# A gated DeltaNet stage: decay sums computed a tile ahead, modulation blocks in four places, inverse blocks moved over two queues

## The chip, the cores and the metric

The kernel runs on one core of a Trainium2 chip. The metric is the device time of one execution in microseconds; before the change the median of three runs is 2671.44 us (2667.06 to 2678.87). Engines: PE or TensorE (matmul), DVE or VectorE, ACT or ScalarE, POOL or GpSimd, SP or SyncE (which issues most DMAs).

## The reference, cut to what matters

One inference step of a two-layer model on 128 context and 512 latent tokens, D_MODEL 1024, float32. Layer 0 mixes by a bidirectional gated DeltaNet (4 heads of 128) beside differential attention, then a dense SwiGLU; layer 1 by latent attention, then experts. Every sub-layer is modulated by vectors `silu(c) @ mod_w + mod_b`. The change touches the DeltaNet and the products with `mod_w`:

```python
g = jnp.cumsum(g, axis=-1)
gdiff = g[..., :, None] - g[..., None, :]
decay = jnp.where(incl, jnp.exp(jnp.where(incl, gdiff, 0.0)), 0.0)
m = jnp.where(strict, jnp.einsum('bhncd,bhnsd->bhncs', kb, k) * decay, 0.0)
a = m + jnp.eye(CHUNK)
sol = lax.linalg.triangular_solve(a, rhs, lower=True, unit_diagonal=True)   # -> u, w
def step(s, inp):                       # over chunks, once forward, once backward
    v_new = u_i - w_i @ s
    o = (q_i * jnp.exp(g_i)) @ s + a_i @ v_new
    s = s * jnp.exp(g_last) + k_dec.T @ v_new
m_s = jnp.split(jax.nn.silu(c) @ mod_w[layer] + mod_b[layer], 6)
```

## The kernel before, in words

The 640 tokens are five tiles of 128 (`NT`), and each tile is one chunk. The inverse of the triangular matrix of each of 2 directions x 5 tiles x 4 heads is made in four steps.

1. *Tile loop* (`pe_delta`, `dve_delta`, `act_delta`, `pool_delta`). GpSimd copies the log decays of a tile over 128 columns (`rows_of`, L1004, one buffer `gb`); TensorE sums them by a product with a triangle ("grow", L1066), transposes keys and values ("tok", L1070 and L1072) and makes both grams ("gram"). VectorE makes the exponents (`exponents`, L1195: L1198, L1203), ScalarE takes exp (L1156), GpSimd multiplies by beta (L1019), and VectorE multiplies into the grams (L1215, L1219); with L1219 the gram's PSUM slot is free. GpSimd also adds up a mask `diag` from ten pieces (L1011, L1012).
2. *Substitution* (`substitute`, L1039). The 32x32 diagonal blocks (4 per matrix, 160 in all) go through DRAM (`z_dram`, L457, then L463) so that each of 80 partitions holds one; VectorE inverts those of direction 0 and GpSimd those of direction 1, in 31 steps of two products (L1046, L1048).
3. *Way back.* The inverses go to `x_dram` (L466, L1024) and come back by `bring_back` (L469, issue at L474), in 20 DMAs of 16 KB for each direction, SyncE's and GpSimd's. VectorE widens them by `diag` (`widen`, L1259), TensorE transposes (`pe_turn`, L1122), and two levels of products (5 and 6) complete the inverse of each tile.
4. *Scan* (`pe_scan`, `dve_scan`), five steps, and the output norm (`pe_onorm` and its partners), then the out projection "eo" with weights `w_eo`.

The order is written out by hand in lists: `TRI` for steps 1 to 3, `STEP` for a scan step. Every entry is one use of a ring of four PSUM slots, in list order; `take` makes TensorE wait until the entry four back was freed, `full` and `done` wait for an entry to be written or freed. An engine runs its own instructions in program order only.

Between them stand the *modulation blocks*: 40 blocks (0 to 39) of 1 MB of `mod_w`. Block b is an entry ("mA", b), eight narrow products of which ScalarE copies the result (L1138), and an entry ("mB", b), a fold and its bias (L1143). Before, blocks 0 to 4 lie in the tile loop, one to a tile, blocks 5 to 29 behind it (`MOD_SCAN` 30), two in each scan step (30 to 39). Their weights come through a ring of five SBUF slots (`WS`), loaded by SyncE in order (L436), each as soon as the block five back was consumed. SyncE's other work hangs on these loads (`carry`, L446): behind load 4 it sends 12 MB of zeros to `rows_dram` (L450), behind loads 4 to 8 a tile's diagonal blocks (L457, eight DMAs), behind load 8 it reads them back (L463), and behind load 22 (`X_BACK`) it waits for the inverse of direction 0, sends it and brings it back. Loads 23 and later wait in program order behind that.

## Time and profile before

| | |
|---|---|
| profiled execution | 2674.86 us (span 2672.9 us) |
| median of three runs | 2671.44 us |
| TensorE busy, whole span | 2367.9 us, 89% |
| VectorE, ScalarE, GpSimd busy | 38%, 32%, 17% |
| DMA | 353.62 MB, mean 132 GB/s |
| tile loop | about 449 to 521 us |
| substitution | 529 to 571 us |
| inverse back, until TensorE's first turn | 571 to 609.5 us |
| levels 5 and 6, and the scan | 609.5 to 749 us |
| output norm, out projection starts | 749 to 763 us |

The profile gives, for one execution, each engine's instructions with start and length, what ended the wait before them, and the DMA issues with their time to landing. Busy time over a whole span says little about a stage in which engines hand work to each other: there one reads who was waited for last. "PEclk" is the granted TensorE clock as a share of the full 2.4 GHz. The ends of matmuls are modelled.

### The profile page before, as it was taken

To read this page: it belongs to the slowest core of one execution; us is meant where nothing else is said; L and a number is where in the kernel's file an instruction comes from. 1 tells how busy PE (TensorE), PEld (TensorE's weight loads), DVE (VectorE), ACT (ScalarE), POOL (GpSimd) and SP (SyncE) were. 2 spreads that over 40 slices of the span, in tenths; PEclk is the share of its full clock that TensorE was granted. 3 is DMA by queue.
4 is the path that set the end of the run, shared out by engine and by line. 5 is a ranking of instruction groups with operands and counts; after the bars stand their busy time and mean duration, and the time that the engine had idled before them with its cause. 6 is when DMAs were issued, how large, how long until landed. Compare 5 with 4: busy or idle time off the path is not lost.

```text
span 2672.9 us, 34343 instructions
## 1 busy us (share of the span) xinstructions
PE 2367.9 (89%) x13870; PEld 1987.9 (74%) x13871; DVE 1005.9 (38%) x1457; ACT 868.2 (32%) x1237; POOL 450.2 (17%) x249
## 2 busy tenths in 40 slices
PE   6999986578888999989989999969898888898994
PEld 3777665447767999989966566769797777797883
DVE  2211264354742222131112333133345766634544
ACT  2211234222104211131122232134335666644544
POOL 0000001273002000020000000024224444433311
PEclk7998988758999999999999999969999999999997
DMA  6111102672310222111211000016448778866755
GB/s 284 49 63 48 40 32 101 212 297 101 134 62 34 81 78 79 65 44 66 107 43 50 17 1 1 0 68 260 165 155 291 292 290 302 321 237 212 264 176 173
DMA packets 72890, 353.62 MB, mean 132 GB/s; under 512 B 15056, under 2 KB 20752, under 8 KB 40112
## 3 DMA queue, kind: packets, MB, share of 16 engines
q1 hardware_dynamic: 68368, 337.94, 34.5%
q0 software_dynamic: 4384, 13.60, 1.4%
q8 instruction: 116, 1.90, 0.3%
q14 instruction: 22, 0.18, 0.0%
HBM read 318.06 MB, written 33.46 MB: 132 GB/s over the span
## 4 chain that ended last, share of the span: by engine, by line
PE 63%; issue 15%; DVE 9%; POOL 7%; ACT 4%; DMA 2%; SPq 1%; POOLq 0%; DVEq 0%; ACTq 0%
PE ps L543 59%; POOL wring_x L1801 5%; PE ps L680 1%; PE ps L898 1%; DVE tmp L1048 1%; ACT arena L950 1%; DVE tmp L1046 1%; DMA xT<-in_x 1%; POOL arena_x L1512 1%; DVE att L920 1%; DVE tmp L1319 1%; DVE tmp L1259 0%; POOL rows L1984 0%; ACT hT L671 0%; DMA wring<-in_w_mod 0%
## 5 line engine op out<-in xcount | busy, mean ns | idle before, releaser
L543 PE MATMUL ps<-hT,wring 128*128 128x320 f32 x1472 | 406.5, 439 | 12.6 <-ACT hT L671 10.6
L543 PEld LDWEIGHTS ps<-hT,wring 128*128 128x128 f32 x1472 | 284.4, 194 | 134.6 <-issue 20.6
L1801 POOL TENSOR_TENSOR wring_x<-wring,arena_x 128x2048 fp32r<-128x2048 f32 (+1 forms) x60 | 276.7, 4619 | 495.6 <-ACT arena_x L1795 495.5
L543 PE MATMUL ps<-arena_x,hT_x 128*128 128x256 f32 x2464 | 330.3, 292 | 21.1 <-issue 21.1
L543 PEld LDWEIGHTS ps<-arena_x,hT_x 128*128 128x128 f32 x2464 | 312.5, 197 | 24.5 <-issue 22.6
L1795 ACT ACTIVATE arena_x<-wring 128x2048 fp32r<-128x2048 f32 x153 | 283.4, 1855 | 90.6 <-DMA wring<-in_w_mgu 89.8
L543 PE MATMUL ps<-arena_x 128*128 128x512 f32 (+2 forms) x1144 | 252.3, 374 | 29.5 <-DVE arena_x L1970 13.3
L1801 DVE TENSOR_TENSOR wring_x<-wring,arena_x 128x2048 fp32r<-128x2048 f32 (+1 forms) x90 | 222.1, 2467 | 73.1 <-ACT arena_x L1795 73.0
L543 PEld LDWEIGHTS ps<-arena_x 128*128 128x128 f32 x1144 | 203.0, 201 | 59.9 <-issue 25.5
L543 PE MATMUL ps<-arena 128*128 128x128 f32 (+3 forms) x680 | 184.3, 434 | 7.0 <-ACT arena L950 4.8
L543 PE MATMUL ps<-wring_x,hT_x 128*128 128x256 f32 x1120 | 151.9, 285 | 5.0 <-POOL wring_x L1801 4.9
L543 PEld LDWEIGHTS ps<-arena 128*128 128x128 f32 (+1 forms) x680 | 107.8, 224 | 62.7 <-issue 48.4
L543 PEld LDWEIGHTS ps<-wring_x,hT_x 128*128 128x128 f32 x1120 | 142.4, 193 | 6.0 <-POOL wring_x L1801 5.7
L543 PE MATMUL ps<-tmp_x,arena_x 128*128 128x320 f32 x832 | 135.3, 315 | 6.0 <-ACT hT L671 6.0
L543 PE MATMUL ps<-hT_x,arena_x 128*128 128x320 f32 x832 | 132.4, 310 | 0.7 <-POOL hT_x L1553 0.7
L543 PEld LDWEIGHTS ps<-tmp_x,arena_x 128*128 128x128 f32 x832 | 127.8, 192 | 6.5 <-issue 6.5
L543 PE MATMUL ps<-tmp_x,wring_x 128*128 128x320 f32 x832 | 131.2, 310 | 0.0
L543 PEld LDWEIGHTS ps<-hT_x,arena_x 128*128 128x128 f32 x832 | 124.9, 188 | 1.0 <-POOL hT_x L1553 1.0
L543 PEld LDWEIGHTS ps<-tmp_x,wring_x 128*128 128x128 f32 x832 | 124.3, 188 | 0.1
L1934 ACT ACTIVATE expf<-ps 128x256 f32<-128x256 f32 x110 | 42.1, 383 | 232.8 <-PE ps L543 232.6
L1406 DVE SCALAR_TENSOR_TENSOR xT<-ps,modcol,xT 128x128 f32<-128x128 f32 (+2 forms) x72 | 27.2, 434 | 226.1 <-PE ps L543 226.1
L2024 DVE TENSOR_TENSOR expf<-expf,ps 128x256 f32<-128x256 f32 x110 | 45.7, 416 | 149.1 <-ACT expf L1934 149.1
(288 smaller groups left out, 2890.9 us busy)
## 6 DMA issues: line engine op xcount, KB each, us to landing
wring<-in_w_mgu SPq DMA_DIRECT2D x105, 1024.0 KB, 6.0
wring<-in_w_mod SPq DMA_DIRECT2D x48, 1024.0 KB, 9.9
wring<-in_w_mdn SPq DMA_DIRECT2D x30, 1024.0 KB, 5.0
wring<-in_w_gu SPq DMA_DIRECT2D x22, 1024.0 KB, 4.8
wring<-in_w_mdn SPq DMA_DIRECT2D x20, 768.0 KB, 4.3
wring<-in_w_ev SPq DMA_DIRECT2D x14, 1024.0 KB, 5.3
rows<-hT SPq DMA_DIRECT2D x1, 12288.0 KB, 33.5
wring<-in_w_dn SPq DMA_DIRECT2D x16, 704.0 KB, 4.2
```

The source lines that it names most:

```text
L543: return nc.tensor.matmul(out, lhsT, rhs, start=first, stop=last)
L680: last = nc.tensor.matmul(pair(s)[:, half, :], ones, tc[:, k, half * HT:(half + 1) * HT], start=(k == 0), stop=(k == KD - 1))
L898: last = nc.tensor.transpose(ps[:, s, n * P:(n + 1) * P], probs(i, 0)[:, n * P:(n + 1) * P], ident)
L920: nc.vector.tensor_reduce(cells(i)[:, st_:st_ + 1], src, AX.X if t == 0 else AX.XY, ALU.max, negate=True).then_inc(mx_ready, 1)
L950: nc.scalar.activation(dst, src, ACT.Exp, bias=cells(i)[:, st_:st_ + 1], accum_out=cells(i)[:, 2 + st_:3 + st_]).then_inc(ps_free[s], 1)
L1046: st.then(eng.tensor_tensor(part, L[:, k + 1:B32, k:k + 1].broadcast_to([NB, rest, n]), X[:, k:k + 1, 0:n].broadcast_to([NB, rest, n]), AL ...
L1048: last = eng.tensor_tensor(X[:, k + 1:B32, 0:n], X[:, k + 1:B32, 0:n], part, ALU.subtract)
L1406: last = nc.vector.scalar_tensor_tensor(xs, ps[:, s, at:at + b - a], modcol[:, bass.ds(c * 2 + (gate * 16 + grp), 1)], xs, ALU.mult, ALU.add)
L1795: nc.scalar.activation(whi[b % 6][:, 0:wsize(b)], wslot[s][:, 0:wsize(b)], ACT.Copy).then_inc(whi_ready, 1)
L1801: eng.tensor_tensor(wslot_x[s][:, 0:size], wslot[s][:, 0:size], whi[b % 6][:, 0:size].bitcast(F32), ALU.subtract).then_inc(ready, 1)
L1934: nc.scalar.activation(sgE[:, j % 2, :, :], pair(s, P), ACT.Silu).then_inc(silu_ready, 1)
L2024: nc.vector.tensor_tensor(actf[:, j % 2, :, :], sgE[:, j % 2, :, :], ps[:, s, :].rearrange("p (m n) -> p m n", m=2)[:, :, P:2 * P], ALU.mu ...
```

## The change

- *Decay sums a tile ahead.* ("grow", t+1) now comes between ("tok", t) and ("gram", t) on TensorE; ScalarE's exp of tile t+1 follows the token copy of tile t; GpSimd copies the rows of tile 1 before it adds up `diag`, and those of tile t+2 behind its beta products of tile t.
- *Modulation blocks over four places.* Two blocks to each tile of the loop (0 to 9), 10 to 24 behind it, 25 to 34 in the scan, and 35 to 39 in a new stage "omod" between the scan and the output norm. VectorE's three `modA` products move behind the norm's own.
- *Transfers.* Of each tile's diagonal blocks SyncE sends direction 0 (behind loads 4, 6, 8, 10, 12) and GpSimd direction 1, four DMAs each; each reads its own direction back, on a semaphore of its own (SyncE behind load 14). The way back has eight DMAs for each direction: for each row group g one of tiles 0 to 3 (64 KB) and one of tile 4 (16 KB), with `compact` laid out to match. `X_BACK` is 27.

```diff
-MOD_SCAN = 30
+MOD_TRI, MOD_SCAN, MOD_END = 10, 25, 35
-X_BACK = 22
+X_BACK = 27
-        TRI = [x for t in range(NT) for x in (("grow", t), ("tok", t), ("gram", t), ("mA", t), ("mB", t))]
-        TRI += [("mA", NT)] + [x for b in range(NT + 1, MOD_SCAN) for x in (("mA", b), ("mB", b - 1))] + [("mB", MOD_SCAN - 1)]
+        TRI = [("grow", 0)]
+        for t in range(NT):
+            TRI += [("tok", t)] + [("grow", t + 1)] * (t < NT - 1) + [("gram", t)]
+            TRI += [(x, 2 * t + b) for x in ("mA", "mB") for b in range(2)]
+        TRI += [("mA", MOD_TRI)] + [x for b in range(MOD_TRI + 1, MOD_SCAN) for x in (("mA", b), ("mB", b - 1))]
+        TRI += [("mB", MOD_SCAN - 1)]
...
+        OMOD = [("mA", MOD_END), ("mA", MOD_END + 1)]
+        for b in range(MOD_END, MODS - MOD_FIRST):
+            OMOD += [("mB", b)] + [("mA", b + 2)] * (b + 2 < MODS - MOD_FIRST)
...
-            if WS - 1 <= j < 2 * WS - 1:
-                t = j - WS + 1
-                done(sync, "tri", prod("gram", t))
-                for d in range(2):
-                    for g in range(4):
-                        sync.dma_start(blocks_of(z_dram, d, t, g), ...).then_inc(z_out, 16)
-            if j == 2 * WS - 2:
-                sync.wait_ge(z_out, 16 * 8 * NT)
-                for d in range(2):
-                    sync.dma_start(zin[d], z_dram[d, :, :]).then_inc(z_in, 16)
+            if WS - 1 <= j < MOD_TRI + WS - 1 and (j - WS + 1) % 2 == 0:
+                blocks_out(sync, (j - WS + 1) // 2, 0)
+            if j == MOD_TRI + WS - 1:
+                blocks_in(sync, 0)
...
+        def blocks_out(eng, t, d):
+            done(eng, "tri", prod("gram", t))
+            for g in range(4):
+                eng.dma_start(blocks_of(z_dram, d, g)[:, t * H:(t + 1) * H, :], ...).then_inc(z_out[d], 16)
+        def blocks_in(eng, d):
+            eng.wait_ge(z_out[d], 16 * 4 * NT)
+            eng.dma_start(zin[d], z_dram[d, :, :]).then_inc(z_in[d], 16)
         def bring_back(eng, d):
             eng.wait_ge(x_out[d], 16)
-            for t in range(NT):
-                for g in range(4):
-                    eng.dma_start(compact(t)[g * B32:(g + 1) * B32, d, :, :], blocks_of(x_dram, d, t, g)
+            for g in range(4):
+                rows, four = slice(g * B32, (g + 1) * B32), 4 * H
+                for at, to in ((slice(0, four), Sst[1][rows, d * 512:(d + 1) * 512]),
+                               (slice(four, NT * H), rstd[rows, 256 + d * P:256 + (d + 1) * P])):
+                    eng.dma_start(to.rearrange("p (n c) -> p n c", c=B32), blocks_of(x_dram, d, g)[:, at, :]
                                   ).then_inc(xc_in[d], 16)
...
             rows_of(0)
+            full(pool, "tri", prod("grow", 0))
+            rows_of(1)
             for i in range(1, 2 * 5):
                 st.then(nc.gpsimd.tensor_tensor(diag, ...))
             for t in range(NT):
-                if t + 1 < NT:
-                    full(pool, "tri", prod("grow", t))
-                    rows_of(t + 1)
                 pool.wait_ge(e_out, t + 1)
                 ...
+                if t + 2 < NT:
+                    full(pool, "tri", prod("grow", t + 1))
+                    rows_of(t + 2)
+                if t:
+                    blocks_out(pool, t - 1, 1)
+            blocks_out(pool, NT - 1, 1)
+            blocks_in(pool, 1)
...
         def act_onorm(act):
-            act.wait_ge(os_ready, 1)
-            nc.scalar.activation(osd[:, :], osd[:, :], ACT.Sqrt, bias=eps, scale=1.0 / P).then_inc(od_ready, 1)
+            for i, (what, b) in enumerate(OMOD):
+                if i == 4:
+                    act.wait_ge(os_ready, 1)
+                    nc.scalar.activation(osd[:, :], osd[:, :], ACT.Sqrt, bias=eps, scale=1.0 / P).then_inc(od_ready, 1)
+                (act_mod_a if what == "mA" else act_mod_b)(act, "omod", i, b)
```

## Rows read from the trace of the kernel before

**Rows 1.** Busy time by stretch: stretch, length, engines' busy us, PEclk, DMA share, GB/s.
```profile
449.00:521.00 72.00, 45.26 (x340) 39.73 (x344) 29.19 (x47) 15.44 (x31) 20.93 (x30) 0.75 0.66 242
469.00:474.00 5.00, 4.35 (x21) 4.35 (x22) 0.60 (x1) 1.02 (x1) 1.41 (x2) 0.50 1.02 410
474.00:479.00 5.00, 4.35 (x41) 3.38 (x40) 0.11 (x1) 0.80 (x3) 0.08 (x1) 0.95 1.03 411
529.00:571.00 42.00, 38.06 (x276) 20.33 (x276) 39.80 (x62) 10.37 (x39) 37.21 (x61) 0.50 0.83 342
571.00:609.00 38.00, 21.46 (x153) 11.86 (x146) 1.49 (x3) 6.13 (x24) 16.70 (x27) 0.50 0.80 289
609.00:749.00 140.00, 121.98 (x1044) 111.14 (x1043) 86.43 (x123) 26.98 (x60) 23.50 (x18) 0.94 0.28 104
```
**Rows 2.** The chain that ended last, 449 to 522 us: start, us, what.
```profile
451.07 3.46 PE ps L543 x16
...
468.40 1.21 DVE arena L1219 x2
...
469.65 1.12 PE ps L1070 x4
...
478.89 1.30 DVE tmp L1198 x2
...
483.96 1.11 PE ps L1070 x4
...
517.82 1.21 DVE arena L1219 x2
```
**Rows 3.** Timeline of GpSimd, first tile: start, us, engine, line, operation.
```profile
450.69 4.70 POOL L1011 TENSOR_TENSOR cst<-cst 128x128 f32<-128x128 f32 x9
...
455.86 1.63 POOL L1006 COPY hT<-dsm 128x512 f32<-128x512 f32 x2
459.26 2.03 POOL L1019 TENSOR_TENSOR arena<-tmp,dsm 128x512 f32<-128x512 f32 x2 [1.77 <-ACT tmp L1156]
```
**Rows 4.** DMA issues, 450 to 484 us: count, KB each, median us to landing.
```profile
rows<-hT SPq DMA_DIRECT2D x1, 12288.0 KB, 33.5
wring<-in_w_mod SPq DMA_DIRECT2D x1, 1024.0 KB, 7.8
```
**Rows 5.** Timeline of SyncE's queue behind the zeros.
```profile
469.62 11.04 SPq L457 DMA_DIRECT2D tri_blocks<-arena  x8
480.71 1.46 SPq L436 DMA_DIRECT2D wring<-in_w_mod  x1
```
**Rows 6.** Timeline, 529 to 612 us, the handovers of the substitution.
```profile
529.11 0.27 DVE L1046 TENSOR_TENSOR tmp<-tmp 80x31 f32<-80x31 f32 x1 [7.59 <-DMA tmp<-tri_blocks]
...
571.13 0.33 SPq L466 DMA_DIRECT2D inv_blocks<-tmp  x1
...
573.87 7.66 SPq L474 DMA_DIRECT2D hT<-inv_blocks  x16
575.77 7.62 POOL L474 DMA_DIRECT2D hT<-inv_blocks  x14 [3.51 <-DMA inv_blocks<-tmp]
...
588.55 1.93 PE L543 MATMUL ps<-wring,rstd 128*32 128x256 f32 x16 [16.17 <-DMA wring<-in_w_mod]
...
594.50 0.69 DVE L1259 TENSOR_TENSOR tmp<-hT,cst 128x512 f32<-128x512 f32 x1 [8.58 <-DMA rstd<-inv_blocks]
...
609.51 1.95 PE L1122 MATMUL ps<-cst,tmp 128*128 128x128 f32 x8
```
**Rows 7.** DMA issues, 440 to 600 us.
```profile
tri_blocks<-arena SPq DMA_DIRECT2D x40, 16.0 KB, 1.8
...
rstd<-inv_blocks POOLq DMA_DIRECT2D x4, 16.0 KB, 6.3
```
**Rows 8.** Timeline around the output norm.
```profile
748.68 0.35 DVE L632 SCALAR_TENSOR_TENSOR modA<-modcol,wsm 128x16 f32<-128x16 f32 x3
...
758.18 3.88 PE L1382 MATMUL ps<-cst,arena 128*128 128x128 f32 x20 [11.41 <-DVE arena L1364]
```

More of the change, by code:

```diff
@@ L1060, in pe_delta, with decay_rows @@
             mm(ps[:, s, 40:80], ones, g_.rearrange("p d t h -> p (d t h)"), True, True).then_inc(ps_full[s], 1)
-            for t in range(NT):
-                a, b = t * P, (t + 1) * P
+            def decay_rows(t):
                 nc.tensor.wait_ge(gb_ready, t + 1)
@@ L1067, in pe_delta @@
                 last.then_inc(ps_full[s], 1)
+            decay_rows(0)
+            for t in range(NT):
+                a, b = t * P, (t + 1) * P
                 s = take("tri", prod("tok", t))
@@ L1073, in pe_delta @@
                 last.then_inc(ps_full[s], 1)
+                if t + 1 < NT:
+                    decay_rows(t + 1)
                 s = take("tri", prod("gram", t))
@@ L1353, in dve_scan @@
                 done(dve, "scan", step(i, 4))
-            done(dve, "scan", step("mB", MOD_SCAN + 2 * NT - 1))
-            dve_modA([1, 2, 3])
             sq = tmp[:, 0:NT * 512]
@@ L1365, in dve_scan @@
                                     spread(osd[:, :], 2, P), ALU.mult).then_inc(on_ready, 1)
+            for what in OMOD[-2:]:
+                done(dve, "omod", OMOD.index(what))
+            dve_modA([1, 2, 3])
             dve.wait_ge(state_out, 16)
```

66 lines of the change are left out of this document (40 added, 26 removed).

## The prediction
> **What bounds the kernel now.** I read the page first (a span of 2672.9 us), then the busy time by stage, because the change touches only the delta stage, about 449 to 763 us [rows 1]. In the tile loop (449 to 521) TensorE is busy 45 of 72 us and VectorE 29, so neither is the bound: they wait in turn. In the substitution (529 to 571) VectorE is busy 39.8 of 42 us and GpSimd 37.2; that is the bound there. From 571 to 609 VectorE is busy 1.5 us and TensorE 21.5 of 38, at clock 0.50, the 1.2 GHz level. From 609 to 749 TensorE and VectorE feed each other again.
>
> The chain of waits shows the loop's turn [rows 2]. After VectorE's last product of tile 0 (starts 468.40, lasts 1.21) TensorE turns the tokens (469.65), makes the gram, two products of a modulation block and only then the next decay sums; VectorE can begin its exponents at 478.89. The same transpose comes again at 483.96: 14.3 us a tile. The last product ends at 517.82 + 1.21 = 519.0. The timeline of the handovers [rows 6] then reads: blocks back for the substitution at 529.11 (10.1 us later), inverse sent at 571.13 (42.0 us), TensorE's first turn of the inverse at 609.51 (38.4 us). In those 38.4 us the inverse is ready much earlier: the last piece of it is widened at 594.50 + 0.69 = 595.2. TensorE is late because seven modulation blocks stand before the turn in its program and their weights were queued behind the wait for the inverse: it sits 16.2 us and starts them at 588.55, 21.0/7 = 3.0 us each.
>
> **The change, part by part.** I follow the five handovers.
>
> *Tile loop, first tile.* Decay sums 0 leave TensorE at 454.5 (451.07 + 3.46 [rows 2]). GpSimd now copies rows 1 (1.63), then does its ten mask additions (4.70 + 0.5), then multiplies beta (2.03) [rows 3]: 454.6 + 1.6 + 5.2 + 2.0 = 463.5, 2.2 later than the 461.3 of before. That is now what VectorE's last product waits for: 463.5 + 1.3 = 464.8, where it was 469.6. The exponents of tile 1 are done by then (sums 1 at about 458 to 459, exponents 2 x 1.3).
>
> *Tiles 1 to 3.* From one last product to the next the order is now: fold of the odd block 0.3 to 0.5, tokens about 2.0 (twice the 1.12 for four at the lower clock, less where it rises), sums of the next tile about 1.9, VectorE's exponents and both products 5.0 (478.89 to 483.9), hops 0.3. That is 9.0 to 10.0; I take 9.5 instead of 14.0 to 14.3. Gram and the two blocks (2 x 1.07, and more at the lower clock) lie beside VectorE's exponents. The last tile has no next sums: 7.0. Ideal end: 464.8 + 3 x 9.5 + 7.0 = 500.3.
>
> *What is late next.* Tile 2 now reads blocks 4 and 5, and block 5 is the first that SyncE loads after the 12 MB of zeros. Those take 33.5 us from 450.32, to 483.8; the block transfers behind them needed 11.04 us to be issued, and block 5, issued at 480.71, landed 7.8 us later, at 488.5 [rows 4, 5]. The earlier gram does not move the zeros. TensorE would want block 5 at 464.8 + 9.5 + 6.5 + 1.1 = 482; with four transfers instead of eight ahead of it, it lands at about 487.5. So 5.5 us are given back: end at 505.8, a gain of 13.2. Blocks 6 to 9 come at 2.6 us each (1.05 MB at the 410 GB/s of 469 to 474 [rows 1]) and are in time. Bounds: 500.3 if block 5 is in time, and 515 if the loop also runs mostly at the lower clock, as in 469 to 474 (0.50, against 0.95 in 474 to 479 [rows 1]), about 2.5 us more in each of four tiles.
>
> *Blocks to the substitution.* SyncE sends four instead of eight (about 1.8 us), waits for landing (1.8 [rows 7]), and issues its one read at about 509.5, but loads 13 and 14 now stand just before that wait: two megabytes, 5.1 us, from about 507.6. The read then lands at about 515 to 516. GpSimd issues its own four: 4 x 0.55 = 2.2 us, landing 2.0 to 6.3 [rows 6, 7], and its read 4 more: 514 to 518. I take 11.0 where before it was 10.1, so 0.9 lost; bounds 8 and 14. Start of the substitution: 516.8. It has the same instructions, 42.0 us: inverse at 558.8. Queued behind GpSimd's earlier sends (4 x 0.55 = 2.2 us in each of tiles 1 to 4) are its next beta products; they are gated by ScalarE's exponent a whole 9.5 us tile apart, and GpSimd's work in that time is 2.0 + 1.2 + 2.2 = 5.4, so they hide. If they did not, 2.2 us a tile, 9 in all.
>
> *Filler under the substitution.* Fifteen blocks (10 to 24) follow the loop: 15 x 3.0 = 45 us, from 506 to 551. The turn can come at about 574. So 23 us of cover; the five blocks taken away from here go two into each tile instead of one and one, and five behind the scan.
>
> *The inverse back.* GpSimd's send and its landing take 4.7 us from the end of the substitution (571.1 to 575.77); its 20 reads of 16 KB are 0.54 us each (7.62/14), and the last landed at 594.5 [rows 6]. Now there are eight reads, four of 64 KB and four of 16 KB. Issue 8 x 0.55 = 4.4, landing 5.3 (between 2.0 alone and 6.3 beside megabyte loads [rows 7]: blocks 28 and 29 go out just behind SyncE's reads, 5.1 us of full engines), widening 0.7: 4.7 + 4.4 + 5.3 + 0.7 = 15.0 us to the turn. SyncE's side needs 2.8 + 8 x 0.48 + 1.9 = 8.5 and is not last. Bounds: 11.7 with an undisturbed landing; 24.1 (571.1 to 595.2, all of before) if a read costs by its 128-byte pieces, whose number is the same. I take the value near the rows of single transfers, because the 12 MB of zeros went out as one transfer too [rows 4]. Before: 38.4. Gain 23.4.
>
> On this a rule of the Trainium skill speaks against the change: in "DMA: Bandwidth & Descriptors", section "Measured (HBM→SBUF, 128 partitions, SWDGE, issued from GpSimd)", transfers under 64 KB are called dominated by their descriptors, and one contiguous run is one descriptor. The pieces stay 128 bytes, 2560 for each direction, so by that rule joining transfers saves little. No row here shows a 64 KB transfer of 128-byte pieces; it is the first rival below.
>
> *Level stage and scan.* 609 to 749 keeps its instructions, and ten blocks stay in the scan: 0. VectorE's copy out of the joined layout has the same shape.
>
> *Behind the scan.* VectorE's three small products (0.35 us at 748.68) leave the path: -0.3. TensorE is idle 11.4 us before 758.18 [rows 8], and five blocks lie there. ScalarE's square root stands in the middle, after four of its ten pieces; after it come about 1.6 us of ScalarE and 1.5 of TensorE, beside VectorE's reciprocal and 2.8 us product. Hidden. Uncovered it would be 5 x 3.0 - 11.4 = 3.6 us. The output weights queue behind these blocks: asked for at about 748, needed 15 us later in shifted time, and two megabytes take 5.1.
>
> Sum: turn at 558.8 + 15.0 = 573.8 against 609.51, 35.7 earlier, and 0.3 behind: 36.0 us. The profiled execution took 2674.86 (span 2672.9 and 1.96 around it), so 2638.9; it lies 3.4 above the median 2671.44 of the runs, so I forecast 2635.
>
> **Rivals.** (A) *The pieces cost, not the transfers.* The way back takes 24.1 instead of 15.0: 9.1 lost, 2644. For it: SyncE and GpSimd both take about half a microsecond for 128 pieces, and no row has more such pieces in one transfer. Against it: the 12 MB of zeros went out as one transfer. Chance 0.15. (B) *The tile loop gains nothing*: block 5 and the lower clock eat 13.2, 2648. For it: 0.50 in 469 to 474; against it: the idle 5 us that precede the low stretch shrink to 2. Chance 0.10; with (A) too, 2657, 0.03. (C) *Everything lands early*: block 5 in time and a landing of 2 us: 5.5 + 3.3 more, 2626. Chance 0.07. (D) *Slower*: TensorE idles some 23 us before the turn, where before it ran without rest since 588. If its clock stayed at 0.50 through 609 to 749, 122 us busy at 0.94 become 229: 107 longer, less 36, 2742. It decides from one third of these 140 us at the lower level. Against it: before, the stage began from 0.50 as well and still has 0.94 as mean [rows 1]. Chance 0.03. (E) *It does not do what it says*, another wait holding the turn as late as now: only 13.2 - 0.9 remains at best, or nothing, 2659 to 2671. Chance 0.04.
>
> A page of the skill would price D differently: "TensorE: Matmul & The Clock Gate", "Part 1: The HAM clock gate", ties the clock to how busy the array has been recently, and busy work follows the idle here as it did in the tile loop, where 0.50 became 0.95 within the next 5 us; by that D costs a few us at most.
>
> **How the numbers follow.** The forecast has 0.58, with its own range 2627 to 2643; A 0.15, B 0.10, A and B 0.03, C 0.07, D 0.03, E 0.04. The range 2624 to 2652 takes in A, B and C and leaves out about 0.15. About 0.5% (13 us) is what a measurement can tell from no change: faster by more, 0.93; within, 0.04; slower, 0.03.
>
> **What would show each step.** In the changed profile: last products 9 to 10 us apart in tiles 1 and 3, a TensorE wait for weights of about 5 us before the second block of tile 2; loop end near 506; substitution from 517 for 42 us; TensorE idle before the turn, released by VectorE's widening; turn near 574, about 15 us after the inverse; the rest shifted whole, the out projection about 36 us earlier. The prediction is wrong if the turn is released by a weight load, if 64 KB reads take over 1 us each to issue, or if the stages behind the turn change in length.

## The result, and the profile after

The changed kernel takes 2654.66 us (median of 20 runs, 2648.14 to 2668.97); the kernel before, on the same chips, 2671.23 (20 runs, 2666.23 to 2692.44). The ratio is 0.9932, its 95% interval 0.9917 to 0.9947. I had forecast 2635 with a range of 2624 to 2652: faster was right, the gain was half of what I had worked out (36 us; by the ratio it is 18), and the time lies 2.7 us above the range. The profiled execution took 2652.94 us, its span 2651.1.

Busy time by stretch, the columns of [rows 1]: tile loop; substitution; the inverse on its way back; level stage and scan; output norm.

```profile
449.00:509.00 60.00, 49.56 (x424) 42.46 (x428) 27.61 (x43) 18.11 (x44) 30.81 (x47) 0.81 0.93 353
...
524.00:567.00 43.00, 28.99 (x204) 16.02 (x204) 36.00 (x52) 8.40 (x32) 37.92 (x62) 0.50 0.72 288
567.00:587.00 20.00, 1.10 (x5) 0.73 (x5) 4.71 (x2) 0.00 (x0) 10.37 (x13) 0.50 0.50 147
587.00:724.00 137.00, 119.29 (x1036) 108.46 (x1036) 86.07 (x120) 25.06 (x55) 23.48 (x18) 0.96 0.24 85
724.00:742.00 18.00, 17.51 (x120) 11.85 (x120) 12.44 (x12) 5.48 (x17) 0.00 (x0) 0.53 0.80 292
```

TensorE was busy 45 of 72 us in the loop before; now it is busy 50 of 60. The way back, 38 us before and half filled with TensorE's blocks, is 20 us of an empty TensorE: the filler is used up, and what is left is the way of the inverse through memory and VectorE's widening at its end. The level stage and scan kept their clock (0.96; 0.94 before).

The timeline of the loop's end and of the blocks' way to the substitution (start, us, engine, line, operation, and in brackets the idle time before and what ended it):

```profile
487.06 1.93 PE L558 MATMUL ps<-wring,rstd 128*32 128x256 f32 x16 [4.99 <-DMA wring<-in_w_mod]
...
505.82 1.28 DVE L1254 TENSOR_TENSOR arena<-ps,arena 128x512 f32<-128x512 f32 x2
507.39 2.18 POOL L474 DMA_DIRECT2D tri_blocks<-arena  x4 [1.71 <-DVE arena L1254]
...
513.22 0.34 SPq L480 DMA_DIRECT2D tmp<-tri_blocks  x1
513.60 7.90 SPq L445 DMA_DIRECT2D wring<-in_w_mod  x5
514.54 0.55 POOL L480 DMA_DIRECT2D tmp<-tri_blocks  x1 [4.97 <-DMA tri_blocks<-arena]
520.54 0.19 DVE L1067 TENSOR_TENSOR tmp<-tmp 80x31 f32<-80x31 f32 x1 [10.96 <-DMA tmp<-tri_blocks]
524.25 0.41 POOL L1067 TENSOR_TENSOR tmp<-tmp 80x31 f32<-80x31 f32 x1 [9.16 <-DMA tmp<-tri_blocks]
```

TensorE waits 4.99 us for the weights of a block at 487.06: this is the wait for block 5 that the prediction named (5.5). At the end two reads of 320 KB are under way, and right behind SyncE's stand megabyte loads of weights. SyncE's read, in front of them, lets VectorE begin after 7.3 us; GpSimd's, issued 1.3 us later, needs 9.7. The substitution is over when its later half is, so GpSimd's start (524.25) counts.

The timeline of the inverse's way back, which answers to [rows 6]:

```profile
561.78 0.33 SPq L467 DMA_DIRECT2D inv_blocks<-tmp  x1
...
567.26 0.57 POOL L1045 DMA_DIRECT2D inv_blocks<-tmp  x1 [0.30 <-POOL tmp L1069]
...
568.36 1.40 SPq L445 DMA_DIRECT2D wring<-in_w_mod  x2
570.56 0.70 POOL L489 DMA_DIRECT2D hT<-inv_blocks  x1 [2.73 <-DMA inv_blocks<-tmp]
...
572.17 1.09 PE L1150 MATMUL ps<-cst,tmp 128*128 128x128 f32 x4 [18.73 <-DVE tmp L1294]
...
580.24 0.66 POOL L489 DMA_DIRECT2D hT<-inv_blocks  x1 [6.00 <-issue]
...
581.46 2.48 POOL L1055 TENSOR_TENSOR tmp<-arena,cst 128x512 f32<-128x512 f32 x2
582.92 4.01 DVE L1294 TENSOR_TENSOR tmp<-hT,cst 128x512 f32<-128x512 f32 x1 [10.89 <-DMA rstd<-inv_blocks]
583.91 2.47 POOL L1055 TENSOR_TENSOR hT<-arena,cst 128x512 f32<-128x512 f32 x2
586.99 1.12 PE L1150 MATMUL ps<-cst,tmp 128*128 128x128 f32 x4 [13.73 <-DVE tmp L1294]
```

Two things stand here that the prediction did not have. Between GpSimd's third and fourth pair of reads its queue stands still for 6.00 us, with nothing in the profile that it waits for ("issue"). And VectorE's widening of the last piece takes 4.01 us, where the same product takes 0.69 in [rows 6]; beside it run GpSimd's mask products.

The handovers of the delta stage, read from the timelines of the two profiles (us; each column is one profiled execution, measured from the first decay sums, so that a shift of everything before them doesn't count):

| stage | before | after | gained | forecast |
|---|---|---|---|---|
| tile loop, to the end of the last product | 67.9 | 57.9 | 10.0 | 13.2 |
| to the later start of the substitution | 10.1 | 17.2 | -7.1 | -0.9 |
| substitution, to GpSimd's send | 42.5 | 43.0 | -0.5 | 0 |
| way back, to ScalarE's copy of the turned inverse | 39.8 | 20.9 | 18.9 | 23.4 |
| levels and scan, to the norm's first product | 137.5 | 135.9 | 1.6 | 0 |
| norm, to the output projection | 14.3 | 18.5 | -4.2 | 0.3 |
| sum | 312.2 | 293.4 | 18.8 | 36.0 |

So the stage gives 18.8 of the 21.8 us by which the two profiled spans differ. The 17.2 us that it is short of the forecast lie in four places: 3.2 in the loop, 6.2 in the handover, 4.5 on the way back, 4.5 behind the scan; the other two rows give 1.1 back.

### The profile page after: what moved, and what is told of

It reads as the page before. It is cut to its first block, busy times and chain, and to the rows that moved or that the text cites. A ratio compares the mean times of both kernels' runs of the same rounds, so it can differ in the third digit from the quotient of the medians.

```text
span 2651.1 us, 34319 instructions
## 1 busy us (share of the span) xinstructions
PE 2358.5 (89%) x13870; PEld 1983.6 (75%) x13871; DVE 1009.2 (38%) x1457; ACT 867.9 (33%) x1237; POOL 456.8 (17%) x258
## 4 chain that ended last, share of the span: by engine, by line
PE 62%; issue 16%; POOL 9%; DVE 6%; ACT 4%; DMA 2%; SPq 0%; POOLq 0%; DVEq 0%; ACTq 0%
PE ps L558 59%; POOL wring_x L1845 5%; PE ps L695 1%; PE ps L913 1%; POOL tmp L1069 1%; ACT arena L965 1%; POOL tmp L1067 1%; POOL arena_x L1556 1%; DMA xT<-in_x 1%; DVE tmp L1354 1%; DVE att L935 1%; DVE tmp L1294 1%; DMA wring<-in_w_mod 1%; POOL rows L2028 0%; ACT hT L686 0%
## 5 line engine op out<-in xcount | busy, mean ns | idle before, releaser
L558 PE MATMUL ps<-arena_x,hT_x 128*128 128x256 f32 x2464 | 328.9, 291 | 20.9 <-issue 20.9
L558 PE MATMUL ps<-arena 128*128 128x128 f32 (+3 forms) x680 | 174.3, 413 | 7.1 <-ACT arena L965 4.8
L558 PEld LDWEIGHTS ps<-arena 128*128 128x128 f32 (+1 forms) x680 | 100.7, 209 | 60.4 <-issue 46.1
```

Of the source, the lines that this page charges most:

```text
L558: return nc.tensor.matmul(out, lhsT, rhs, start=first, stop=last)
```

## The experiments

The expectations name their theories by letters. Q: transfers that GpSimd sends are late because SyncE's megabyte loads fill the same 16 DMA engines. P: a transfer costs by its 128-byte pieces, whoever is beside it. R: GpSimd's own queue of transfers under way is full.
Outside the delta stage the profiles differ by up to 17 us from kernel to kernel (1903 to 1920 us from the output projection to the end) with no part of the program changed there, so the stage table, one profiled execution of each kernel, is the sharper reading, and the ratio shows whether a gain reaches the end. By the ratio alone only the four edits together are clear of the changed kernel on the fast side, and the blocks spread and the transfers on the slow side; the intervals of all others overlap its own. The loop with two blocks takes 58 or 60 us in kernels that don't differ there; below 2 us it tells nothing. Same columns as above, us; "one" is one modulation block to each tile:

| kernel | loop | in | subst. | back | scan | norm | sum | median, ratio to before (95%) |
|---|---|---|---|---|---|---|---|---|
| after | 57.9 | 17.2 | 43.0 | 20.9 | 135.9 | 18.5 | 293.4 | 2654.66, 0.9932 (0.9917 to 0.9947) |
| loads held on the way in | 60.1 | 9.1 | 42.7 | 21.5 | 136.9 | 14.3 | 284.6 | 2645.42, 0.9915 (0.9877 to 0.9952) |
| loads held on the way back | 59.8 | 17.3 | 42.9 | 16.6 | 137.0 | 14.3 | 287.9 | 2650.06, 0.9927 (0.9899 to 0.9956) |
| SyncE reads both back | 58.0 | 17.4 | 42.6 | 10.1 | 136.4 | 18.5 | 283.1 | 2644.14, 0.9889 (0.9859 to 0.9919) |
| twenty reads | 57.9 | 17.2 | 42.6 | 26.8 | 139.7 | 14.7 | 299.0 | 2661.64, 0.9958 (0.9941 to 0.9974) |
| masks first | 59.5 | 16.9 | 42.9 | 18.3 | 136.5 | 18.4 | 292.6 | 2650.26, 0.9912 (0.9888 to 0.9936) |
| zeros early | 51.0 | 16.5 | 42.5 | 22.3 | 136.1 | 15.6 | 284.1 | 2646.20, 0.9901 (0.9881 to 0.9921) |
| one block | 43.3 | 20.7 | 40.9 | 20.8 | 135.8 | 18.5 | 280.0 | 2644.95, 0.9909 (0.9879 to 0.9938) |
| no blocks behind the scan | 59.9 | 17.8 | 42.6 | 23.6 | 139.9 | 14.3 | 298.2 | 2662.50, 0.9934 (0.9906 to 0.9962) |
| before + sums ahead | 43.6 | 13.0 | 42.6 | 39.6 | 136.2 | 14.7 | 289.7 | 2654.83, 0.9935 (0.9916 to 0.9955) |
| before + blocks spread | 67.9 | 10.0 | 42.6 | 29.7 | 137.2 | 14.4 | 301.8 | 2663.92, 0.9971 (0.9953 to 0.9988) |
| before + transfers | 67.7 | 12.7 | 42.4 | 29.8 | 136.2 | 14.7 | 303.5 | 2666.22, 0.9977 (0.9964 to 0.9990) |
| four edits together | 43.6 | 8.7 | 42.6 | 21.4 | 137.3 | 14.5 | 268.1 | 2630.77, 0.9851 (0.9829 to 0.9874) |

### Loads held on the way in

```diff
-            if j == MOD_TRI + WS - 1:
+            if j == MOD_TRI + WS - 3:
                 blocks_in(sync, 0)
+                for d in range(2):
+                    sync.wait_ge(z_in[d], 16)
```

> The changed kernel, but SyncE reads the blocks back right behind its last send and holds loads 13 and later until both directions have landed. Theory Q: from the last product of the tile loop to the first step of the substitution 9 to 10 us in both directions, instead of 13.4 and 17.1; TensorE's blocks have room for the later loads, so the span is 5 to 7 us shorter. Theory P or a slow GpSimd queue by itself: GpSimd's direction stays at 14 us or more.

SyncE now issues its read before loads 13 and 14, and no load until both reads have landed. The timeline of the two reads and the two starts:

```profile
514.02 0.32 SPq L482 DMA_DIRECT2D tmp<-tri_blocks  x1
514.10 0.55 POOL L482 DMA_DIRECT2D tmp<-tri_blocks  x1 [2.13 <-DMA tri_blocks<-arena]
517.49 0.19 DVE L1069 TENSOR_TENSOR tmp<-tmp 80x31 f32<-80x31 f32 x1 [5.51 <-DMA tmp<-tri_blocks]
...
518.55 0.29 POOL L1069 TENSOR_TENSOR tmp<-tmp 80x31 f32<-80x31 f32 x1 [3.90 <-DMA tmp<-tri_blocks]
```

GpSimd's read takes 4.5 us from its issue to the first step instead of 9.7, its wait for its own sends 2.13 us instead of 4.97, and the handover 9.1 us instead of 17.2. The transfers are the same, with the same pieces; only their neighbours are gone. That is Q, and worth 8 us. The edit both puts SyncE's read before loads 13 and 14 and holds the later ones, and this run doesn't part the two. Of the 8.8 us in its sum, 4.2 are the shorter norm, which the hold doesn't explain, and the loop is 2.2 longer.

### Loads held on the way back

```diff
                 bring_back(sync, 0)
+                sync.wait_ge(xc_in[1], 16 * 8)
```

> The changed kernel, but SyncE waits for GpSimd's way back before it loads blocks 28 and 29 (they are not asked for before the scan). Theory Q (the megabyte loads delay GpSimd's reads): landing of the 64 KB reads falls from 6.6 to about 2.5 us, the stop of 6.0 us falls under 2, the widening of direction 1 starts 5 to 6 us sooner after the end of its substitution (10 instead of 15.9). Theory R alone (its queue is too short whatever the engines do): the stop stays above 4. Theory P: the stop and the landing stay as they are.

No load is issued between the reads of direction 0 and the landing of direction 1. The timeline:

```profile
568.99 0.57 POOL L1046 DMA_DIRECT2D inv_blocks<-tmp  x1 [0.30 <-POOL tmp L1070]
...
577.64 0.66 POOL L490 DMA_DIRECT2D hT<-inv_blocks  x1 [1.74 <-issue]
...
580.28 4.06 DVE L1295 TENSOR_TENSOR tmp<-hT,cst 128x512 f32<-128x512 f32 x1 [8.63 <-DMA rstd<-inv_blocks]
```

From the send to the start of the widening it takes 11.3 us instead of 15.7, and the stop in GpSimd's issues shrinks from 6.00 to 1.74. The first three reads of 64 KB land 2.4 us after their issue (median) instead of 6.6. The traces also have each transfer's landing, and they show what ends the stop: the last of the six reads under way lands at 577.26 here and at 579.86 after, and GpSimd issues its next 0.38 us later in both. Each of the 23 stops of this kind in the kernels of the table and the kernel before ends 0.37 to 0.48 us after the last of GpSimd's own transfers has landed. So the queue stops until it is empty, and the loads beside it set how long that takes: Q and R hold together, and R alone (a stop above 4) does not. Whether more room would do away with the stop is not shown. The 4.06 us of the widening stay.

### SyncE reads both directions back

```diff
                 bring_back(sync, 0)
+                bring_back(sync, 1)
...
-            bring_back(pool, 1)
```

> The changed kernel, but SyncE issues the reads of the way back of both directions, eight and eight; GpSimd only sends its own inverse. Theory R (GpSimd's queue of descriptors is full) and theory Q (megabyte loads beside it) agree here: no stop and no load ahead, the widening of direction 1 starts about 9 us after GpSimd's substitution ends (3.3 for the send, 8 x 0.46, 2.1) instead of 15.9. Theory P (the pieces cost by themselves, whoever issues them): 14 or more.

The timeline:

```profile
567.06 0.57 POOL L1046 DMA_DIRECT2D inv_blocks<-tmp  x1 [0.30 <-POOL tmp L1069]
567.65 2.49 POOL L1055 TENSOR_TENSOR tmp<-arena,cst 128x512 f32<-128x512 f32 x2
568.98 4.15 DVE L1294 TENSOR_TENSOR tmp<-hT,cst 128x512 f32<-128x512 f32 x1 [8.02 <-DMA rstd<-inv_blocks]
...
575.30 0.69 DVE L1294 TENSOR_TENSOR tmp<-hT,cst 128x512 f32<-128x512 f32 x1 [2.17 <-DMA rstd<-inv_blocks]
```

The way back falls to 10.1 us, half of the changed kernel's and a quarter of before's. Three costs go with one edit, and this run doesn't part them: the stop, the loads ahead (they stand behind the reads in SyncE's own queue), and the slow product, since GpSimd's masks now run while direction 1 is still under way. It meets the first widening instead, which has slack.

### Twenty reads in the changed kernel

```diff
-                for at, to in ((slice(0, four), ...), (slice(four, NT * H), ...)):
+                for t in range(NT):
```

> The changed kernel with 20 reads of 16 KB a direction on the way back instead of eight. Theory of transfers (what costs is the number of reads, 0.48 to 0.55 us each): SyncE's side 5.6 us later (widening of direction 0 at about 15 instead of 9.5 us after its send), GpSimd's issue 12 x 0.55 = 6.6 us longer; but the two megabyte loads then come after most of its reads, so the widening of direction 1 moves by 0 to 3 us only. Theory P (the 128-byte pieces cost, their number is the same): both directions as in the changed kernel within 1 us.

Same bytes, same 128-byte pieces, 20 transfers for each direction instead of eight. The timeline:

```profile
566.81 0.57 POOL L1045 DMA_DIRECT2D inv_blocks<-tmp  x1 [0.30 <-POOL tmp L1069]
...
570.11 2.23 POOL L489 DMA_DIRECT2D hT<-inv_blocks  x4 [2.73 <-DMA inv_blocks<-tmp]
...
583.71 0.55 POOL L489 DMA_DIRECT2D rstd<-inv_blocks  x1 [5.97 <-issue]
...
588.30 4.15 DVE L1294 TENSOR_TENSOR tmp<-hT,cst 128x512 f32<-128x512 f32 x1 [12.98 <-DMA rstd<-inv_blocks]
```

Four reads of 16 KB take 2.23 us of GpSimd, one of 64 KB with the same 512 pieces 0.66 to 0.70. The way back is 5.9 us longer; the expectation had given direction 1 only 0 to 3. P, which is rival A, is false: transfers cost, pieces hardly. (Without loads beside them, in the kernel above, 64 KB land in 2.4 us and 16 KB in 1.9, so the 384 pieces more cost 0.5 us there and 0.1 in the issue.)

### Masks first

```diff
-            bring_back(pool, 1)
             pool.wait_ge(x_ready[0], 1)
+            # the first two mask products of level 5 here
+            bring_back(pool, 1)
```

> The changed kernel, but GpSimd makes its first two mask products (2.5 us) while its inverse is on the way to memory, before it issues the reads back. In the changed kernel VectorE's widening of direction 1 takes 4.0 us instead of 0.7 while GpSimd's mask products run. Theory S (the two engines' products slow each other when they run at once): the widening takes 0.7 us when it starts after the remaining two products, or about 2 if it overlaps their end; the turn comes 2 to 4 us sooner. Rival (the long product is waiting for its data, which the record does not show): it stays 4 us. If the reads are issued later by the products, at most 0 to 2.5 us is lost ahead.

The timeline of the second half of the way back:

```profile
581.89 2.48 POOL L1059 TENSOR_TENSOR hT<-arena,cst 128x512 f32<-128x512 f32 x2
583.24 1.69 DVE L1298 TENSOR_TENSOR tmp<-hT,cst 128x512 f32<-128x512 f32 x1 [11.77 <-DMA rstd<-inv_blocks]
```

The run of mask products beside the widening is two instead of four, and the widening takes 1.69 us. So it does not wait for its data, which was the rival. The way back is 2.6 us shorter (18.3); 2.3 of them are this product (4.01 to 1.69). The stop in front of it stays, at 5.90.

### Zeros early

```diff
-  spread(Sst[0], 1, 2 * ITEMS)).then_inc(y_rows_out, 16)
+  spread(arena[:, 24576:25600], 1, 2 * ITEMS)).then_inc(y_rows_out, 16)
```

(The source is cleared before the attention's first part, so the 12 MB of zeros are on their way before the delta stage begins.)

> The changed kernel, but the 12 MB of zeros are written from another zeroed tile about 100 us earlier, under the attention, and the 0.9 us memset ahead of the delta stage is gone from the path. If the wait for block 5 comes from the zeros, as predicted: no wait for weights in the tile loop, its tiles 9.5 to 10.5 us apart throughout, the last product about 7 us sooner after the first decay sums (51 instead of 58), the span 6 to 8 us shorter than the changed kernel's. If the loads are late for another reason (SyncE held by its block transfers), a wait above 2 us stays. If the zeros delay something under the attention, that stage grows by up to the same amount.

No wait for weights is left in the loop. VectorE's last products of two tiles, from the timeline:

```profile
469.91 1.28 DVE L1254 TENSOR_TENSOR arena<-ps,arena 128x512 f32<-128x512 f32 x2
...
479.96 1.28 DVE L1254 TENSOR_TENSOR arena<-ps,arena 128x512 f32<-128x512 f32 x2
```

The loop is 51.0 us instead of 57.9, so late weights cost 6.9. But the tiles still follow each other by 10.05 us: what is left there is no wait for weights. What it is, the three parts alone show below.

### One block to each tile

(With `MOD_TRI` 5, and SyncE's sends behind loads 4 to 8 as in the kernel before.)

```diff
-            TRI += [(x, 2 * t + b) for x in ("mA", "mB") for b in range(2)]
+            TRI += [("mA", t), ("mB", t)]
```

> The changed kernel with one modulation block in each tile of the loop (0 to 4, and 5 to 24 behind it) instead of two; everything else of the change stays. Theory L (the second block makes TensorE the bound of the loop, and brings the wait for block 5): the loop takes 44 to 46 us from the first sums to the last product, as with the sums alone (44.1), instead of 58.4; the substitution starts 12 to 14 us sooner. TensorE has 20 blocks under it, 56 to 60 us from 494, and is done at about 553; the turn comes at about 565 to 570, so nothing is lost there if the weights are in time. Span 2634 to 2642, 10 to 17 us under the changed kernel. Rival theory F (the second block was needed as filler: the 20 blocks hold the turn, or their loads stand beside the way back): TensorE's idle time before the turn under 1 us, or the turn less than 8 us sooner than in the changed kernel, span 2645 or more.

The loop takes 43.3 us, 14.6 less, with the zeros where they are: no tile then reads block 5. That is what L said, and F is out: the copy of the turned inverse comes 13.4 us sooner after the first sums, where F allowed 8. The median, 2644.95, is still outside the 2634 to 2642 expected. What is won is partly lost at once: the handover becomes 20.7, because GpSimd's sends follow each other at a faster pace and stand for 5.13 us, and its read again has the loads beside it. The timeline of VectorE's and GpSimd's starts:

```profile
499.00 3.26 POOL L473 DMA_DIRECT2D tri_blocks<-arena  x6 [5.13 <-issue]
...
504.25 0.19 DVE L1066 TENSOR_TENSOR tmp<-tmp 80x31 f32<-80x31 f32 x1 [4.82 <-DMA tmp<-tri_blocks]
...
517.61 0.60 POOL L1066 TENSOR_TENSOR tmp<-tmp 80x31 f32<-80x31 f32 x1 [9.24 <-DMA tmp<-tri_blocks]
```

### The three parts alone, on the kernel before

Sums ahead (the order of the changed kernel with one block to each tile):

```diff
-        TRI = [x for t in range(NT) for x in (("grow", t), ("tok", t), ("gram", t), ("mA", t), ("mB", t))]
+        TRI = [("grow", 0)]
+        for t in range(NT):
+            TRI += [("tok", t)] + [("grow", t + 1)] * (t < NT - 1) + [("gram", t), ("mA", t), ("mB", t)]
```

> The kernel before with the decay sums a tile ahead and nothing else: one block a tile, all transfers on SyncE. Theory of the sum (each gain passes on to the next handover): tiles 9.5 to 10 us apart instead of 14, the loop's last product 48 to 50 us after the first sums instead of 68, handovers behind it unchanged, span 16 to 20 us shorter. It has no wait for block 5 in the loop, since block 5 stands behind it. Rival (TensorE still late at the turn because of blocks 23 to 29, whose loads stand behind the inverse): these loads move with the inverse, so the same gain; if they did not, the turn would stay near 609 and the gain vanish.

Blocks spread (five in the loop as before, 20 behind it, 10 in the scan, 5 behind the scan):

```diff
-MOD_SCAN = 30
+MOD_TRI, MOD_SCAN, MOD_END = 5, 25, 35
-X_BACK = 22
+X_BACK = 27
```

> The kernel before with the modulation blocks spread and nothing else: one in each tile, 20 behind the loop (5 to 24), 10 in the scan, 5 behind it, and SyncE waits for the inverse behind load 27. TensorE no longer holds the turn, which then follows the widening of direction 1. In the kernel before that came at 594.5, with five megabyte loads beside its reads; now two stand beside them, so 590 to 595 and the turn at 591 to 596 instead of 609.5: 14 to 19 us. Behind the scan 0 to 4 us are lost, by TensorE's clock there. Span 11 to 18 us shorter. If the blocks' weights are late anyway, less than 8.

Transfers (two queues and fewer, larger reads back; everything else as before):

```diff
-                for d in range(2):
-                    for g in range(4):
-                        sync.dma_start(blocks_of(z_dram, d, t, g), ...).then_inc(z_out, 16)
+                blocks_out(sync, j - WS + 1, 0)      # direction 1: blocks_out(pool, t - 1, 1)
```

> The kernel before with the transfers changed and nothing else (two queues, eight reads back for each direction). The turn still waits for blocks 23 to 29, whose loads are issued behind SyncE's reads: these go out about 5.5 us sooner with 8 instead of 20 reads, so the turn comes 4 to 5.5 us sooner. The substitution starts 0 to 3 us later or sooner (no loads stand before SyncE's read here). Theory Q: GpSimd's reads of the way back meet seven loads and land 3 us or more later than in the changed kernel, but ahead of the turn, so it costs nothing. Span 2 to 6 us shorter.

The stage gains are 22.5, 10.4 and 8.7 us: 41.6 if they added up, and 18.8 together. The sums alone take as much time as the whole change (0.9935 against 0.9932). Their loop is shorter than expected (43.6 for 48 to 50), and 2.9 us of it are lost in the handover, which was to stay as it was.

With one block tiles are 7.4 us apart. With two they are 9.9 to 10.1 apart (zeros early, and 472.94 to 483.06 after). So the second block costs 57.9 - 43.6 = 14.3 us in the loop: 6.9 that it reads block 5 too soon, and 7.4 in the pace of the tiles. The timelines of one tile show where these lie: ScalarE's exp, the fold of the last block, the next sums, and VectorE's next exponents. First after, then the sums alone:

```profile
471.86 1.06 ACT L1184 ACTIVATE tmp<-tmp 128x1024 f32<-128x1024 f32 x1 [4.91 <-DVE tmp L1238]
...
474.36 0.58 PE L558 MATMUL ps<-cst,hT 128*128 128x2 f32 x4 [0.52 <-DVE arena L1254]
...
475.71 3.58 PE L558 MATMUL ps<-cst,hT 128*128 128x128 f32 x16
...
479.32 1.29 DVE L1233 TENSOR_TENSOR tmp<-ps,dsm 128x512 f32<-128x512 f32 x2 [5.11 <-PE ps L558]
```

```profile
477.82 1.06 ACT L1165 ACTIVATE tmp<-tmp 128x1024 f32<-128x1024 f32 x1 [3.42 <-DVE tmp L1217]
...
479.21 0.61 PE L545 MATMUL ps<-cst,hT 128*128 128x2 f32 x4 [1.28 <-ACT hT L1147]
...
480.58 1.95 PE L545 MATMUL ps<-cst,hT 128*128 128x128 f32 x16
...
482.57 1.29 DVE L1212 TENSOR_TENSOR tmp<-ps,dsm 128x512 f32<-128x512 f32 x2 [2.38 <-PE ps L545]
```

The busy time over the sums, with the granted clock as the third number from the end, in the same order:

```profile
475.70:479.20 3.50, 3.50 (x19) 3.50 (x18) 0.00 (x0) 1.02 (x1) 0.00 (x0) 0.51 1.02 357
```

```profile
480.60:482.50 1.90, 1.90 (x20) 1.90 (x19) 0.00 (x0) 1.02 (x1) 0.40 (x1) 1.00 0.90 185
```

Of the 2.7 us between the two kinds of tile, 1.1 lie before the sums (3.85 us from the start of the exp, against 2.76). A tile with two blocks has seven entries in the ring of four slots, so its second fold takes the slot of that tile's gram and must wait for VectorE's last product (0.52); the fold itself takes the rest. With one block there are five entries, that slot falls to the next sums, and they don't wait for it. The other 1.6 us are the sums themselves, 3.58 at a clock of 0.51 against 1.95 at 1.00. Why the clock is low there is not shown; just before, TensorE rests 0.42 and 0.52 us in the tile with two blocks, and 1.28 us in the one with one. The gram and the two blocks are not on this path: in the tile of the first fence they run from 469.00 to 472.81, beside VectorE's exponents and products (469.22 to 474.22). So L is right that the block costs the loop, but not by TensorE's load.

The two other parts share one piece of path: each alone brings the way back to about 30 us, and only both give 20.9. With the blocks spread, the inverse is late: three loads are issued just before the two sends, GpSimd's send lands after 8.6 us instead of 3.5, and 20 reads follow. The turn came 4 us after the latest time expected, and the median gained 8 us instead of 11 to 18. With the transfers changed, both sides are late. TensorE has its blocks in front, and beside the twelve loads that follow SyncE's reads GpSimd's send takes 7.2 us and its reads stop for 8.38. The last piece is widened at 600.33, and TensorE, which has turned the first half by then, waits 0.91 us for it. The expectation had that piece land ahead of the turn.

### No blocks behind the scan

```diff
-MOD_TRI, MOD_SCAN, MOD_END = 10, 25, 35
+MOD_TRI, MOD_SCAN, MOD_END = 10, 30, 40
-X_BACK = 27
+X_BACK = 29
```

> The changed kernel, but the last five modulation blocks are not behind the scan: 20 instead of 15 blocks under the substitution, 10 in the scan, none behind. In the changed kernel 4 us were lost between the end of the scan and the out projection, where the blocks stand (square root 1.9 us late behind ScalarE's pieces, TensorE 2.0 us late with the last block, on the lower clock). If the blocks cause it: out projection 15.8 us after the scan's last state update, as before, instead of 19.8, span 3 to 5 us shorter. If 20 blocks are too many before the turn (20 x 3.0 = 60 us from 507 to 567, turn at 587): no loss there. If they are not hidden, TensorE's idle time before the turn is under 1 us and the turn comes later.

The norm is 14.3 us again, 4.2 less than after. But more blocks stand before the turn, and their megabyte loads run beside the way back (23.6; the piece of direction 1 is widened 21.7 us after its send), the stage of the levels is 4.0 longer and the loop 2.0: a loss of 4.8 in sum, where a gain of 3 to 5 was expected. GpSimd's queue stops for 8.25 us here, with five loads beside it instead of two. Why the levels take longer is not shown. The ratio, 0.9934, tells no difference from the changed kernel: that the place behind the scan, which costs up to 4.2 us, is still the cheaper one stands on this one profile.

### Four edits together

One block to each tile, loads held on the way in, zeros early, SyncE reads both back; the edits are those above.

> The changed kernel with four edits together: one block in each tile, SyncE holding its later loads until the blocks of both directions are in, the 12 MB of zeros written under the attention, and SyncE issuing the way back of both directions. If the measured gains add: 14 (loop) + 7 to 8 (handover in) + 1 to 3 (memset and queue) + 11 (way back), about 33 us under the changed kernel, 2618. The zeros' own 6.9 us is mostly in the loop's 14 already. If TensorE's 20 blocks become the bound (loads begin only at about 500, 20 x 2.8 = 56 to 60 us, last at 555 to 560, turn wanted at about 550): 5 to 10 us of it are lost, 2622 to 2630.

2630.77 us (2627.59 to 2635.20), ratio 0.9851, better than both kernels, the changed one by some 0.8%. It is 13 us short of the 2618 expected, and the timeline shows where most of it is:

```profile
548.18 0.61 SPq L468 DMA_DIRECT2D inv_blocks<-tmp  x1
...
556.58 0.33 SPq L491 DMA_DIRECT2D hT<-inv_blocks  x1
...
565.99 0.69 DVE L1291 TENSOR_TENSOR tmp<-hT,cst 128x512 f32<-128x512 f32 x1 [3.34 <-DMA rstd<-inv_blocks]
```

Three megabyte loads stand in SyncE's queue right in front of its send of direction 0 (issued from 542.19 to 548.13), so that it goes out later than GpSimd's (546.52). It then takes 8.4 us until it has landed and the first read is issued, where it took 2.7 (561.78 to 564.44) after. So the way back is 21.4 us, not 10.1: by what the holds above showed, and by the late send of the blocks spread, the same cause in another place. It isn't TensorE's 20 blocks, which are done at 555.2. A version that holds those loads too was not run.

## Why the prediction was half right

**Tile loop.** The sums a tile ahead are the part that works: they release VectorE's exponents early, as I had read from the chain [rows 2], and the gram and the blocks do lie beside VectorE's work, as I had said. What failed are the sizes of the terms, 54.7 us foreseen and 57.9 measured:

| term | foreseen | measured |
|---|---|---|
| to the end of the first tile | 13.7 | 14.9 |
| three tiles without late weights | 3 x 9.5 | 10.1, 10.1 and 9.9 (the last from zeros early) |
| late weights, block 5 | 5.5 | 6.8 |
| last tile | 7.0 | 6.0 |

In the first tile GpSimd's mask additions took 6.6 us instead of 5.2, beside VectorE's products. In each of the three, "sums of the next tile about 1.9" is the term: 3.6, at the lower clock, while the tokens, taken as 2.0, took 0.9; so 9.5 is near by luck. And the second block, which I had laid in as free filler, was never set against one block: it costs 14.3 of the loop's 57.9 us. Without it the sums alone are worth the whole change. Rival B, that block 5 and the lower clock eat the loop's 13.2, came a quarter true: 3.2.

**Handover in.** Foreseen 11.0, measured 17.2. The failing step is "and its read 4 more": GpSimd's read took 9.7 us to GpSimd's first step, which is 5.7 of the 6.2 missing. Its four sends took 5.0 to land, within my 2.0 to 6.3. I had seen that loads 13 and 14 stand before SyncE's read and had not asked what the loads behind it do to a read on the other queue. With them held, it is 9.1. The bound of 14 was too low: both a transfer alone (1.8) and one beside megabyte loads (6.3) stood in [rows 7], and I gave the read 4.

**Substitution.** 43.0 measured, 42.0 foreseen (42.5 before, read in the same way): as said.

**Filler.** It lasted to about 553.4, 18.7 us before the first half turned, and 33.5 before the second, which is the half that counts; foreseen was 551, and 23 to the turn. The end of the filler was right.

**Way back.** 15.0 foreseen from the send to the second half of the turn, 19.7 measured (567.26 to 586.99); my four terms add up to 15.1:

| term | foreseen | measured |
|---|---|---|
| send and landing | 4.7 | 3.3 |
| eight reads | 4.4 | 4.9 + stop of 6.0 |
| landing of the last, from the end of its issue | 5.3 | 1.5 |
| widening | 0.7 | 4.0 |

The failing steps are "8 x 0.55 = 4.4", which puts the queue's stop of 6.0 at nothing, and "widening 0.7", which took 4.0 beside GpSimd's mask products. The landing was overrated, and the errors cancel in part. The total lies half way to rival A's 24.1, but not by its cause. Holding the loads takes 4.3 of it away (20.9 to 16.6), fewer mask products 2.6, SyncE as reader 10.8. For rival A I had weighed a page's rule: "DMA: Bandwidth & Descriptors", section "Measured (HBM→SBUF, 128 partitions, SWDGE, issued from GpSimd)", of the Trainium skill, calls transfers under 64 KB dominated by descriptors. The trace does not bear out the use that the rival made of it: a transfer of four times the pieces takes 0.66 us of GpSimd instead of 0.57 and, with no loads beside it, lands in 2.4 instead of 1.9; and joining saved 5.9 us.

**Levels and scan.** 137.5 to 135.9, nothing, as said. Rival D did not happen: after 18.7 us of idleness and a stage at 0.50, TensorE's clock is 0.96 over 587 to 724.

**Behind the scan.** "Hidden" was wrong: 4.2 us lost, and even the 3.6 given as "uncovered" is exceeded. The square root comes 1.9 us late behind ScalarE's pieces, and TensorE 2.0 late with the last block. With the five blocks and the norm's own products TensorE is busy 17.5 of 18 us at 0.53, the blocks 2.8 us apart; where the clock is 0.88 in the same stretch with the same blocks, they are 1.5 apart and the loss is nil. Busy time there, with the blocks in both: loads held on the way back, then one block.

```profile
722.60:736.90 14.30, 11.65 (x121) 8.70 (x121) 12.54 (x12) 5.15 (x17) 0.00 (x0) 0.88 0.83 336
```

```profile
715.10:733.60 18.50, 17.49 (x120) 11.86 (x121) 12.83 (x12) 5.47 (x17) 0.00 (x0) 0.54 0.76 284
```

So it was hidden at one clock and uncovered at the other. Which one a kernel gets did not follow from any edit I made here: after, SyncE as reader, masks first and one block had 0.53 to 0.54; both kernels with held loads, the combination and the blocks spread on the kernel before had the short norm (14.3 to 14.5); twenty reads and zeros early lie between (14.7 and 15.6, at 0.79 and 0.78). This stays open.

**As a whole.** The direction and the place were right, the loop's chain too, and two of the six lengths (substitution, levels and scan, within 1.6). The sum was double because most costs were taken from rows in which the resource was free: the DMA engines, GpSimd's queue, VectorE's operands, TensorE at the full clock. The largest single cause is SyncE's loads beside GpSimd's transfers: holding them back returned 8.1 and 4.3 us. And the sum never asked what each part is worth alone, where one part is worth all of it.

## What to carry to other kernels

Before filler is counted as free in a loop that hands over through a ring of slots, count the entries again: one entry more can put a take behind the slowest reader. Then price the work on the path at both clocks, since here the same sums took 1.95 and 3.58 us. A small transfer moved to a second queue gains little while the first queue fills the DMA engines; what has to be held back is the bulk load beside it. On the way back one queue for both directions, with the loads behind, took half the time of two. Parts that shorten the same stretch don't add: measure them alone, and one of them may be worth all of it.

## What the hardware showed that I had not expected

**A VectorE product can stand through several of GpSimd's.** The widening reads two operands from SBUF and takes 0.69 us alone. Started while GpSimd made four mask products back to back, it took 4.01 to 4.15 us in seven kernels, and with two products 1.69 and 1.74; each time it ended 0.55 to 0.57 us after the last product of GpSimd's run (after: 586.93, the run over at 586.38; SyncE as reader: 573.13 and 572.57; masks first: 584.93 and 584.37). The Trainium skill, in "SBUF — State Buffer", section "SBUF: two separate sides", says that the two engines share a port pair under an exclusive lock, which one of them holds for its whole instruction. The trace agrees that one blocks, but one mask product is 1.24 us, and VectorE waited through up to three in a row: it did not get its turn between two of them. It is not always so. At the widening of the next tile, in every kernel, VectorE's second product starts 0.6 us into the first of GpSimd's two, takes 1.76 us and ends 0.55 us after that first one (601.33 and 600.78 after), and GpSimd's second takes 1.72 us: there VectorE did get its turn. What decides between the two is not shown.

**The substitution may have the same cause in small.** With GpSimd 13.4 us behind (one block), VectorE's 31 steps took 37.2 us (504.25 to 541.48) instead of 41.2 after (520.54 to 561.76), where GpSimd starts 3.7 us behind. That the shared products are the reason is argued, not shown.

**A busy TensorE at the low clock.** In the substitution TensorE is busy 38 of 42 us before and 29 of 43 after, and its granted clock stays at 0.50, the 1.2 GHz level, in both kernels; in the level stage, busy 119 of 137, it is at 0.96.

**A queue that stops until it is empty.** On the way back GpSimd's issues stand for 8.38, 8.25, 7.37, 6.53, 6.00, 5.97, 5.90, 5.86 and 1.74 us in the nine kernels with the transfers changed in which GpSimd reads its own direction back, and for 1.9 to 2.0 us in the three with the transfers of the kernel before, with no releaser in the profile, and in the one pair that differs in nothing else (6.00 and 1.74) the stop is shorter where SyncE loads nothing beside it. Every one of them ends 0.37 to 0.48 us after the last of GpSimd's own transfers has landed. On the way back the stop comes behind 14 reads of 16 KB, or behind three of 64 KB and three of 16 KB: 1792 and 1920 pieces of 128 bytes. That would let the room go by pieces and not by transfers, but no run was made for it.
